# Two-layer hybrid decoder step on one core: samples interleaved with the prompt pairs, pooling slabs ahead of value slabs, two blocks' bounds summed by the scalar engine

## The reference

```python
def multiscale_pool(ext, pos):            # windows 2, 4, 8, 16 over 4 groups of 128 channels
    ... outs.append((end[..., sl] - start) / cnt)
    return mean - ext[:, POOL_HIST:]      # then one 128x128 product a group, and a scale

def index_select(qi, wi, ki_all, pos_q, k_sel):
    dots = relu(einsum('nthd,nsd->nths', qi, ki_all))
    score = einsum('nth,nths->nts', wi, dots)
    score = where(arange(S)[None, :] <= pos_q[:, None], score, -inf)
    _, idx = top_k(score, k_sel)          # 256 of up to 1024 keys (prompt), 129 of 516 (samples)
    return idx

def sparse_attend(q, ks, vs, idx, pos_q): # 8 heads of 64, softmax over the chosen keys
    ...
```

## Time and profile before

| | us |
|---|---|
| median of three timed runs | 2890.39 (2887.62 to 2892.45) |
| the profiled execution | 2893.66 |
| its span in the trace | 2891.9 |
| busy in the span: PE, PEld, DVE, ACT, POOL | 2606.2, 2417.4, 1413.3, 861.2, 1020.3 |
| mean granted clock of TensorE | 0.942 of 2.4 GHz |

### The profile page before, as it was taken

The page is one execution under the profiler, slowest core; times in us unless marked ns, Lnnn a source line. Parts: engine busy times, 40 slices in busy tenths (PEclk is TensorE's granted clock), DMA queues, the critical chain, the costliest instruction groups (busy, mean ns, idle before and its releaser), DMA issues.

```text
span 2891.9 us, 42127 instructions
## 1 busy us (share of the span) xinstructions
PE 2606.2 (90%) x15608; PEld 2417.4 (84%) x15608; DVE 1413.3 (49%) x1783; ACT 861.2 (30%) x1370; POOL 1020.3 (35%) x752
## 2 busy tenths in 40 slices
PE   7899979999999999879998586689799999999995
PEld 7899969999999999768688123469699999999995
DVE  2522265555155155342757868551654552542534
ACT  3211143122122122342841125651531221221223
POOL 2222663433233234812842300006534333332355
PEclk9999979999999999889999786899799999999997
DMA  3111101211111111132120340001012111111111
GB/s 127 38 38 50 37 28 44 73 44 44 59 46 47 60 44 46 54 74 61 36 84 29 126 127 15 1 16 44 29 44 73 44 51 53 49 51 51 44 54 70
DMA packets 66988, 152.07 MB, mean 53 GB/s; under 512 B 7978, under 2 KB 32106, under 8 KB 66634
## 3 DMA queue, kind: packets, MB, share of 16 engines
q1 hardware_dynamic: 58816, 134.05, 15.7%
q10 hardware_dynamic: 8074, 16.75, 1.9%
HBM read 137.15 MB, written 10.11 MB: 51 GB/s over the span
## 4 chain that ended last, share of the span: by engine, by line
PE 75%; issue 8%; DVE 8%; ACT 3%; POOL 3%; DMA 1%; SPq 1%; POOLq 1%; DVEq 0%; ACTq 0%
PE PS L490 23%; PE PS L493 23%; PE PS L491 22%; DVE mark L1676 2%; POOL WL L1211 1%; PE PS L744 1%; POOL SCT L1327 1%; ACT PR L1131 1%; POOL Z L1277 1%; PE PS L699 1%; PE PS L755 1%; ACT PT L1148 1%; PE PS L677 1%; DVE pe L1767 1%; PE PS L720 1%
## 5 line engine op out<-in xcount | busy, mean ns | idle before, releaser
L491 PE MATMUL PS<-XL,WH 128*128 128x352 f32 x3168 | 1027.4, 325 | 0.0
L490 PE MATMUL PS<-XH,WH 128*128 128x352 f32 x2976 | 969.1, 326 | 34.0 <-POOL WL L1211 19.4
L1211 POOL TENSOR_TENSOR WL<-RAW,WH 128x1024 fp32r<-128x1024 f32 x210 | 525.8, 2505 | 1021.6 <-ACT WH L834 1021.5
L493 PE MATMUL PS<-XH,WL 128*128 128x352 f32 x2976 | 647.4, 326 | 0.0
L490 PEld LDWEIGHTS PS<-XH,WH 128*128 128x128 f32 x2976 | 566.4, 190 | 60.8 <-issue 42.0
L491 PEld LDWEIGHTS PS<-XL,WH 128*128 128x128 f32 x3168 | 601.6, 190 | 0.0
L493 PEld LDWEIGHTS PS<-XH,WL 128*128 128x128 f32 x2976 | 514.6, 190 | 0.0
L834 ACT ACTIVATE WH<-RAW 128x1024 fp32r<-128x1024 f32 x210 | 223.4, 1064 | 602.6 <-PE PS L493 586.2
L490 PE MATMUL PS<-HH,WH 128*128 128x352 f32 x1056 | 341.0, 324 | 17.9 <-POOL WL L1211 13.9
L491 PE MATMUL PS<-HL,WH 128*128 128x352 f32 x1056 | 340.5, 323 | 0.0
L1464 DVE SCALAR_TENSOR_TENSOR cv<-ext,fpar,cv 128x1072 f32<-128x1072 f32 x88 | 287.6, 3268 | 12.3 <-DVE cv L1460 0.2
(11 more groups left out here) (253 smaller groups left out, 3029.5 us busy)
## 6 DMA issues: line engine op xcount, KB each, us to landing
RAW<-in_slabs SPq DMA_DIRECT2D x210, 512.0 KB, 3.6
KP<-in_ck SPq DMA_DIRECT2D x32, 256.0 KB, 3.4
VP<-in_cv SPq DMA_DIRECT2D x32, 256.0 KB, 2.9
out_o_y<-Z ACTq DMA_DIRECT2D x6, 704.0 KB, 3.3
Z<-in_xT ACTq DMA_DIRECT2D x4, 528.0 KB, 8.9
Z<-in_xT SPq DMA_DIRECT2D x4, 528.0 KB, 10.5
out_o_k<-K ACTq DMA_DIRECT2D x1, 2112.0 KB, 9.9
kix<-in_kidx SPq DMA_DIRECT2D x32, 64.0 KB, 1.9
```

Source lines behind the costliest of these rows:

```text
L490: pe.matmul(o, WH[j][:, k, :], hi[:, k, c * TW:(c + 1) * TW], start=first, stop=False)
L491: pe.matmul(o, WH[j][:, k, :], lo[:, k, c * TW:(c + 1) * TW], start=False, stop=False)
L493: mm = pe.matmul(bank_set(j)[:, c, :], WL[j][:, k, :], hi[:, k, c * TW:(c + 1) * TW], start=False, stop=last)
L1211: pool.tensor_tensor(WL[j][:, :, :], RAW[j][:, :, :], WH[j][:, :, :].bitcast(F32), ALU.subtract).then_inc(w_lo, 1)
```

## The change

The order of layer 1's mixer is rewritten. Pooling slabs come ahead of the value slabs (`S_P` = 14, `S_V` = 18), POOL makes the window adds, the pooled products go between the chunks of the value slabs. The samples go two at a time in 64 rows, with their steps placed at fixed pairs of the pair loop (`LOGITS_AT`, `TURN_AT`, `VALUES_AT`, `OUT_AT`); all logits are one pair ahead, in banks 0 and 1, since the samples have 2 and 3. DVE bisects blocks 2 to 5 in one group; blocks 6 and 7 are bisected with ACT summing the signs of score minus candidate (`sign_sums`) and DVE setting the candidates (`next_bound`), and their last bit is checked for rounding (`last_bound`). Buffers move accordingly (`qf`, `QB`, page buffers, `skeep`, `smark`). The core of the diff:

```diff
-        S_KI, S_WI, S_QI, S_K, S_Q, S_V, S_P, S_END = 0, 1, 2, 6, 10, 14, 18, 22
+        S_KI, S_WI, S_QI, S_K, S_Q, S_P, S_V, S_END = 0, 1, 2, 6, 10, 14, 18, 22
-        GROUPS = ((2, 3, 4), (5, 6, 7))
-        slab_rounds = {9: 0, 10: 12, 11: 13, 12: 13, 13: 13, 14: 9, 15: 9, 16: 9, 17: 8, 18: 5, 19: 5, 20: 4, 21: 3}
-        slot_rounds = [7] * 8 + [3] * 13 + [0] * 19
+        SPAIRS = SEQS // 2
+        LOGITS_AT, TURN_AT, VALUES_AT, OUT_AT = {4: 1, 8: 2, 11: 3}, {0: 0, 5: 1, 9: 2, 12: 3}, {2: 0, 6: 1, 10: 2, 13: 3}, {7: 0, 14: 1}
+        OWN, SIGNED = (2, 3, 4, 5), (6, 7)
+        PASSES = 32 * len(OWN)
+        STEPS = 31
+        slab_rounds = {9: 0, 10: 7, 11: 11, 12: 11, 13: 9, 14: 6, 15: 8, 16: 8, 17: 8, 18: 8, 19: 7, 20: 7, 21: 6}
+        pair_rounds = [6] + [5] * 6 + [0] * 25
+        slab_signs = {15: 2, 16: 3, 17: 3, 18: 3, 19: 2, 20: 3, 21: 3}
+        pair_signs = [0] + [1] * 12 + [0] * 19
...
 @block.sync
+            sp.wait_ge(pooled, 4)
+            sp.wait_ge(pst_set, 4)
             key_pages(0)
+            sp.wait_ge(w_lo, OUT1)
+            sp.dma_start(rep[:, :, :], io["rep"]).then_inc(rep_in, 16)
+            sp.wait_ge(z_up, 4)
             value_pages(0)
+            for j in range(1, SPAIRS):
+                sp.wait_ge(slg, j)
+                key_pages(j)
+                sp.wait_ge(spv, j)
+                value_pages(j)
...
 @block.tensor
+            slabs(IN1 + S_P, 4, KD, XH, XL)
+            products = {(0, 0): (0, False), (0, 2): (0, True), (0, 4): (1, False), (0, 6): (1, True),
+                        (1, 2): (2, False), (1, 5): (2, True), (2, 2): (3, False), (2, 5): (3, True)}
+            for c in range(4):
+                slab(IN1 + S_V + c, KD, XH, XL,
+                     between=lambda k, c=c: pooled_product(*products[c, k], max(0, c - 1)) if (c, k) in products else None)
+                if c:
+                    turn_values(c - 1)
+            turn_values(3)
...
+                for c in range(4):
+                    for x in range(2):
+                        o = PS[rows.start + 32 * x:rows.start + 32 * x + 32, 2, :]
+                        pe.matmul(o, QB[:, c, 2 * j + x, :], KP[x][:, c, :], start=(c == 0), stop=False)
...
+            sample_logits(0)
+            logits(0)
             for p in range(PAIRS):
-                if ahead(p):
-                    logits(ahead(p))
+                if p + 1 < PAIRS:
+                    logits(p + 1)
+                if p in LOGITS_AT:
+                    sample_logits(LOGITS_AT[p])
+                if p in TURN_AT:
+                    sample_turn(TURN_AT[p])
+                if p in VALUES_AT:
+                    sample_values(VALUES_AT[p])
+                if p in OUT_AT:
+                    sample_values_turn(OUT_AT[p])
                 turn_probs(p, 0)
                 turn_probs(p, 1)
...
 @block.scalar
+            def sign_sums(at):
+                for st, x in signs(at):
+                    n = P * (SIGNED[x] + 1)
+                    act.wait_ge(scand, 2 * st + x + 1)
+                    if st + x:
+                        act.wait_ge(signed, 2 * st + x)
+                    act.activation(smark[:, 0:n], SC[SIGNED[x]], ACT.Sign, bias=cand[:, 4 + x:5 + x].bitcast(F32),
+                                   accum_out=cnt[:, 4 + x:5 + x]).then_inc(signed, 1)
+            for g in range(4):
+                pooled_input(g)                  # g = 0 also copies the query blocks QB
+                sign_sums(S_P + 1 + g)
+            for c in range(4):
+                for g in ((0, 1), (2,), (3,), ())[c]:
+                    pooled_scaled(g)
+                n = IN1 + S_V + c
+                act.wait_ge(mm_done, n + 1)
+                act.activation(three(qf[n % 2][:, :]), bank_set(n % 2), ACT.Copy).then_inc(evac_done[n % 2], 1)
+                if c < 2:
+                    split_high(n + 2)
+                if c < 3:
+                    sign_sums(S_V + 1 + c)
...
 @block.gpsimd
+                split_rest(n + 2)
+                while width < w:
+                    pool.tensor_tensor(o[:, lo:PEXT], a[:, lo:PEXT], a[:, lo - width:PEXT - width], ALU.add).then_inc(pwin, 1)
...
 @block.vector
+            def next_bound(st, x):
+                bit, n = STEPS - 1 - st, P * (SIGNED[x] + 1)
+                dve.wait_ge(signed, i + 1)
+                dve.tensor_scalar(rej[:, 4 + x:5 + x], cnt[:, 4 + x:5 + x], float(2 * TOPK_P - 1 - n), 2.0 ** bit, ALU.is_ge, ALU.mult)
+                dve.scalar_tensor_tensor(cand[:, 4 + x:5 + x], rej[:, 4 + x:5 + x], 3 << (bit - 1) if bit else 1, cand[:, 4 + x:5 + x], ...)
+            slab_best(S_P)
+            for g in range(4):
+                slab_best(S_P + 1 + g)
+                pooled_rows(g)
+            for c in range(4):
+                if c < 3:
+                    slab_best(S_V + 1 + c)
+                value_rows(c, 25 + 3 * c)
...
             for p in range(PAIRS):
                 if n:
                     row_max(n, 0)
                     row_max(n, 1)
+                if p in LOGITS_AT:
+                    sample_max(LOGITS_AT[p])
+                rounds(p, 0)
                 if n:
                     row_recip(n, 0)
                     row_recip(n, 1)
                 if p >= 2:
                     att_rest(p - 2)
+                rounds(p, 1)
+                if p in LOGITS_AT:
+                    sample_recip(LOGITS_AT[p])
+                if p in (14, 15):
+                    last_bound((14, 15).index(p))
```

More of the change, by code:

```diff
@@ L703, in sample_turn, with pooled_product @@
-            def sample_turn(s):
-                pe.wait_ge(snorm, s + 1)
-                if s >= 1:
-                    pe.wait_ge(ste, 2 * s)
+            slabs(IN1 + S_P, 4, KD, XH, XL)
+            def pooled_product(g, last, turns):
+                pe.wait_ge(pooled, g + 1)
+                pe.wait_ge(turn_evac, 2 + 25 + 3 * turns)
+                if last:
+                    pe.wait_ge(c_kept, 2 * g + 1)
+                    pe.matmul(PS[:, 6, 0:TW], cw[:, g, :], PL[:, g, 2 * TW:3 * TW], start=True, stop=True).then_inc(cmm, 1)
+                else:
+                    if g:
+                        pe.wait_ge(c_kept, 2 * g)
+                    for c in range(2):
+                        mm = pe.matmul(PS[:, 6 + c, 0:TW], cw[:, g, :], PL[:, g, c * TW:(c + 1) * TW], start=True, stop=True)
+                    mm.then_inc(cmm, 1)
@@ L719, in sample_values @@
                 for t in range(4):
[L720 to L721 removed]
+                    for x in range(2):
+                        o = PS[rows.start + 32 * x:rows.start + 32 * x + 32, 2, :]
+                        pe.matmul(o, spt[:, t, 32 * x:32 * x + 32], VP[x][:, t, :], start=(t == 0), stop=False)
+                pe.matmul(PS[rows, 2, :], spt[0:NS, 4, :], VS[:, :], start=False, stop=True).then_inc(spv, 1)
@@ L1114, in sample_out, with sample_kept @@
+            def sample_kept(j):
+                rows = srows(j)
+                act.wait_ge(spv, j + 1)
+                if j >= 2:
+                    act.wait_ge(sv_turned, 1)
+                act.activation(skeep[rows, :], PS[rows, 2, :], ACT.Copy).then_inc(sv_kept, 1)
             def sample_out(g):
@@ L1346, in _ @@
             pool.wait_ge(phist_in, 16)
-            for g in range(4):
+            step = 0
+            for g, w in enumerate((2, 4, 8, 16)):
                 n = IN1 + S_P + g
@@ L1714, in slab_best, with mixed @@
+            def mixed(own, mine):
+                for k in range(max(len(own), 1)):
+                    if own:
+                        best(own[k])
+                    n = max(len(own), 1)
+                    for st, x in mine[k * len(mine) // n:(k + 1) * len(mine) // n]:
+                        next_bound(st, x)
             def slab_best(s):
                 a = sum(n for x, n in slab_rounds.items() if x < s)
-                for u in range(a, a + slab_rounds[s]):
-                    best(u)
+                mixed(list(range(a, a + slab_rounds[s])), signs(s) if s in slab_signs else [])
```

563 lines of the change are left out of this document (271 added, 292 removed).

## The result

The changed kernel takes 2836.84 us (median, 2836.08 to 2837.33), the kernel before 2889.05 beside it: a ratio of 0.9817, with a 95% interval of 0.98 to 0.9834, a gain of 52.2 us. The forecast was 2852 and a gain of 38.6. So the direction and the range held, and 14 us more came than the steps gave. What follows asks which steps were off, by how much, and where two errors cancelled.

A forecast was written before the change was run, and what follows sets the result against it. Pages, DVE's counts and DVE's choices were taken to end one after another. Steps brought pair 17's maximum from 1835.5 to 1796.9, a gain of 38.6 us: 2855.1 profiled, 2852 against medians; two in ten lie outside 2812 to 2882.

The forecast's parts named there:

- the forecast's own sign of being wrong: Pairs 0 to 13 taking much more or less than 145 us together, or values ending far from 1620.
- C: Pairs 0 to 6, paced by DVE's counts and choices: 76 us (64 to 91), ending at 1703.5.
- D: Pairs 7 to 13, paced by ACT, with sample products standing out: 69 us (50 to 80), ending at 1772.5.
- E: Pairs 14 and 15, DVE's last bounds with rounding check and choices: 24.4 us, ending at 1796.9.
- A: Pooling, then value slabs, after the last query slab: TensorE held behind ACT's scaling, free for samples at 1620.5 (1611 to 1636).
- rival 2: Sign needs its own table: two 1.28 us loads a pair, six pairs pay 15.4 us, 2868; chance 0.07.
- Anchor: Left: last query slab's end, 1481.2, nothing ahead depending on the order. Right: pair 17's row maximum, 1835.5, unchanged from there.
- B: Start of the samples, two as one unit: logits 4.6 us, pages hidden, pair 0's loop beginning at 1627.5.
- Everything fits: Sample products and POOL's adds stay under DVE and ACT: 40 us less, 2812; chance 0.18.
- Sign has its own table: Two table loads of 1.28 us in each of twelve pairs, six pairs paying 15.4 us: 2868; chance 0.07.
- POOL and DVE block each other: Window adds at 3.9 us, small DVE operations waiting: slabs grow 15 us, samples' start 6, 2873; chance 0.05.
- Pairs in series: One pair of logit banks makes engines run in series in pairs 0 to 13: 49 us more, 2901; chance 0.08.

The follow-up runs named there:

- experiment 1: Kernel before the change, with DVE's first count waiting until block 5 is scored too: 2889.18 against 2890.46 us, ratio 0.9997.
- experiment 7: Changed kernel with the 62 sign passes and DVE's small steps behind them left out: 2808.26 against 2890.19 us, ratio 0.9719.
- experiment 6: Changed kernel with three quarters of the sample products left out for sequences 2 to 7: 2823.58 against 2890.19 us, ratio 0.977.

## Why the prediction was right, and where it was not

The total came out right in direction and range, 13.6 us better than forecast. By the forecast's own sign of being wrong, pairs 0 to 13 taking much less than 145 us, it was not right in the pairs: they took 127.7, with C and D each inside its bounds. Some of its sums are slightly off, and none moves the account: DVE's terms in C add up to 62.7, not 62, the terms of E to 23.7, not 24.4, the 1511.6 in A is 1 us more than the terms named with it, rival 2 comes to 2867, and the chances for faster add up to 0.89.

**Anchor.** "Nothing ahead of it depends on the new order" holds. What I took for a difference of 4.5 us was one execution against another (experiment 1). The forecast sum was made against the profiled execution of before, which started late, with 3.3 us taken off; that was about the right correction. The anchor on the right holds within the mixer (84.7 us from pair 17 to 31, 84.6 before), and 2.3 us are lost behind it.

**A: right in mechanism and nearly in size** (135.6 for 139.3). TensorE stands 20.8 us in the first value slab, behind ACT's scaling, behind six sign passes. The four steps up to the scaling came up to 3.4 us off each, both ways: group 0 after 28.9 us instead of 32.3, group 1 after 15.2 and group 2 after 16.9 instead of 17.2 each, the scaling 15.2 after group 2 instead of 12.8. The 3 us counted for the clock behind the hold had no row; they came: after the 20.8 us of standing still TensorE was granted 0.50 of its full clock, the lower of its two levels, from 1553.9 to 1560.0; at the upper level the same work would have taken some 3.0 us less. These rows, of ACT, TensorE and DVE in order of time, show the chain: the last pass, the scaling, the product, and DVE held by a sign that is queued on ACT behind the slab's emptying.

```profile
1551.78 1.15 ACT L1103 ACTIVATE smark<-SCT,cand 128x1024 bf16<-128x1024 f32 x1 [1.61 <-DVE cand L1784]
1552.84 0.19 ACT L1103 ACTIVATION_READ_ACCUMULATOR smark<-SCT,cand 128x1 f32 x1
1552.93 0.83 ACT L1091 ACTIVATE PL<-PS,csc 128x704 f32<-128x704 f32 x1
...
1553.90 1.51 PE L698 MATMUL PS<-PL,cw 128*128 128x352 f32 x2 [20.83 <-ACT PL L1091]
...
1569.65 0.15 DVE L1780 TENSOR_SCALAR rej<-cnt 128x1 int32<-128x1 f32 x1 [12.54 <-ACT smark L1103]
```

I saw the hold and priced it, but didn't say what it means: A would be 23 us shorter without signs (experiment 7), so the change pays for ACT's counts in the one stretch that was TensorE's.

**B: right.** The sixteen logit products of two samples took 3.63 us and the whole unit 4.6; no page was waited for. What I had left out is ACT's table load ahead of the sample exponential, 1.28 us, and DVE's sample maximum, 0.72 us, together about the 1.9 that are missing.

**C: right in mechanism, DVE's own work over-sized.** DVE was busy 56.9 us where I had 64, its idle time 10.1 where I had 12. A step over four blocks took about 3.6 us instead of 3.96, and two next_bounds take 0.53 us together, not 1.0, as here behind pair 8's maximum in the changed kernel:

```profile
1688.96 0.14 DVE L1780 TENSOR_SCALAR rej<-cnt 128x1 int32<-128x1 f32 x1
1689.15 0.16 DVE L1784 SCALAR_TENSOR_TENSOR cand<-rej,cand 128x1 int32<-128x1 int32 x1
1689.23 0.15 DVE L1780 TENSOR_SCALAR rej<-cnt 128x1 int32<-128x1 f32 x1
1689.41 0.16 DVE L1784 SCALAR_TENSOR_TENSOR cand<-rej,cand 128x1 int32<-128x1 int32 x1
```

I had taken the 0.5 from a step's two small instructions with the gaps ahead of them.

**D: the step that failed.** I added the signs (2.2 us a pair, 13 in all) to ACT's passes, and put TensorE's sample products on top (21), as if ACT were busy and waiting in turn. The products do stand out (experiment 6), but the signs lie mostly beside them (experiment 7: 3.3 us). 69 less the 10 us that are counted twice is 59, and 61 was measured. That the 21 for the products was nearly right is luck: I had taken a product for 8.7 us and let ACT's signs and norms cover 3.5 of it. The four units of D took 6.5, 6.0, 4.7 and 5.6 us, 22.7 in all, and of the 12.6 us that experiment 6 took off their main matmuls 12.1 had stood out.

**E: right.** Both last bounds stand in front of a row maximum: 13.2 and 12.8 us for the two pairs, 26.0 for 24.4.

**The rivals.** *Everything fits* fell: experiment 6 found 16 us in the open for three quarters of six sample products. *Sign has its own table* fell: ACT's groups of the changed kernel from 1477 to 1760 us hold 62 sign passes, at 1.04 and 1.15 us for the two sizes, and one load, ahead of the first sample exponential.

```profile
L1103 ACT ACTIVATE smark<-SCT,cand 128x896 bf16<-128x896 f32 (+1 forms) x62 | 67.8, 1094 | 19.9 <-DVE cand L1784 17.0
...
L1135 ACT ACT_TABLE_LOAD x1 | 1.3, 1283 | 8.2 <-DVE ssm L1899 8.2
```

By the Trainium skill, "ScalarE: Activation LUTs", section "Table sets: the hidden batching unit", every change of set costs a load; the trace agrees with the condition on which the forecast's sum stood, that Sign asks for no load of its own: 38 of the passes ran ahead of that one load and 24 behind it, among the exponentials. *POOL and DVE block each other* was half right: they do, but the price falls on DVE (last section), and A came out 3.7 us shorter than forecast, not 15 longer; how much of DVE's price lay on the path no run shows. *Pairs in series* (2901) fell: with one pair of logit banks the narrow pairs took 66.8 and 60.9 us in sevens, less than forecast. Yet the wait that it names, logits behind the exponential, is the largest of TensorE's now (40.0 us up to pair 17).

## What to carry to other kernels

Before a busy engine's work is given to an idle one, look for the stretch in which each piece will stand: a sign step (two passes) cost some 0.6 us in the pairs, mostly beside a wait for TensorE (6.7 us for 12 steps), and 1.2 us among slabs that TensorE paces (23 us for 19 steps), where ACT's next scaling was queued behind it. Two terms on two engines, of which one runs while the other waits, are one term, the larger; adding them made the largest error of a single term here, 10 us. And before explaining a few us, compare two traces ahead of the first changed instruction.

## What the runs showed of the hardware

Nine of GpSimd's ten window additions took 2.17 to 2.18 us beside DVE's counts and small operations, and the tenth 2.67; beside DVE's long two-input work GpSimd's additions had been slower. Here DVE's small operations waited instead. GpSimd's groups of the changed kernel from 1477 to 1612 us, and two lines of DVE over the whole span (duration min/median/max in ns):

```profile
L1406 POOL TENSOR_TENSOR pe<-pe 128x1190 f32<-128x1190 f32 x4 | 8.7, 2176 | 0.0
```
```profile
L1722 DVE TENSOR_SCALAR rej<-cnt x32: 169/170/2043, 1427.0 to 1667.8; 128x4 int32<-128x4 f32 x32
...
L1780 DVE TENSOR_SCALAR rej<-cnt x62: 135/148/155, 1497.3 to 1740.7; 128x1 int32<-128x1 f32 x62
```

A 1190-wide addition took 2.18 us, where I had counted 2.8 to 3.9. Of 106 small DVE operations in that stretch (the steps behind counts and signs) 16 took 1.13 to 2.09 us, together 20 us over their usual 0.16. Each of the 16 began while GpSimd was in an addition or a split and ended 0.01 to 0.03 us behind it, as in the first two, here of GpSimd and then of DVE:

```profile
1490.48 2.40 POOL L1250 TENSOR_TENSOR WL<-RAW,WH 128x1024 fp32r<-128x1024 f32 x1 [0.54 <-ACT WH L853]
1492.83 2.17 POOL L1406 TENSOR_TENSOR pe<-pe 128x1190 f32<-128x1190 f32 x1
```
```profile
1491.77 1.13 DVE L1722 TENSOR_SCALAR rej<-cnt 128x4 int32<-128x4 f32 x1
1492.93 2.09 DVE L1728 SCALAR_TENSOR_TENSOR cand<-rej,cand 128x4 int32<-128x4 int32 x1
```

It met those with two inputs and the four-wide operation with one. The one-wide operation with one input (L1780) never waited so: ten of its 62 ran inside an addition or a split and took 0.14 to 0.16 us. The Trainium skill, "GPSIMD Engine Reference", section "Specifications", names two SBUF inputs, or a mode in which DVE uses both its ports, as the condition: the first fits the rows, and whether the second is what holds the four-wide operation no run here shows.
